# Three plain chunks per FFN instead of four, parts of 8, 7 and 7 chunks, and two of four weight mixtures formed by accumulating DMAs

## The reference

```
def swiglu(x, g, w_gu, w_down):           # D_FF = 2816 = 22 chunks of 128
    gu = rmsnorm(x, g) @ w_gu             # w_gu: 1024 x 5632
    return (silu(gu[..., :D_FF]) * gu[..., D_FF:]) @ w_down
x = x + swiglu(x, g_ffn[i], w_gu[i], w_down[i])
```

## Time and profile before

| | |
|---|---|
| median of the runs | 1291.03 us |
| the profiled execution's own time | 1293.6 us |
| its span | 1291.9 us |
| TensorE, VectorE, ScalarE, GpSimd busy | 98%, 63%, 46%, 3% |
| granted TensorE clock, mean | 0.995 of full speed |
| DMA engines' mean rate over the span | 89 GB/s |

### The profile page before, as it was taken

How to read it: one execution, slowest core, us unless ns; L and a number is a source line. 1 busy time by engine, 2 the same in 40 slices (tenths; PEclk the granted TensorE clock), 3 DMA queues, 4 the chain that set the end, 5 groups by cost and what they waited for, 6 DMA issues and landing times. The chain is left out here.

```text
span 1291.9 us, 23175 instructions
## 1 busy us (share of the span) xinstructions
PE 1260.4 (98%) x9420; PEld 1218.7 (94%) x9420; DVE 819.5 (63%) x1344; ACT 589.3 (46%) x1078; POOL 37.8 (3%) x60
## 2 busy tenths in 40 slices
PE   6999999999999999999999999999999999999997
PEld 6998999999999999999998986799999999999997
DVE  4765557964885588654654466556874786378741
ACT  6656435431552255434663467534451454155421
POOL 1000000000000000002000100000000000000011
PEclk8999999999999999999999999999999999999999
DMA  6234122232323233324443320022233223223321
GB/s 214 83 117 131 33 82 82 66 101 80 96 85 99 65 99 98 98 82 131 130 115 101 102 70 2 2 82 82 66 105 89 75 85 111 86 75 99 115 77 46
DMA packets 201969, 114.92 MB, mean 89 GB/s; under 512 B 5035, under 2 KB 198219, under 8 KB 201864
## 3 DMA queue, kind: packets, MB, share of 16 engines
q1 hardware_dynamic: 197832, 101.24, 26.6%
q0 software_dynamic: 3840, 12.15, 2.5%
q10 hardware_dynamic: 192, 0.06, 0.0%
HBM read 106.54 MB, written 6.90 MB: 88 GB/s over the span
## 5 line engine op out<-in xcount | busy, mean ns | idle before, releaser
L961 ACT ACTIVATE WH<-RAW 128x1024 fp32r<-128x1024 f32 (+2 forms) x157 | 161.2, 1027 | 271.3 <-PE ACCP L1553 271.2
L1246 DVE TENSOR_TENSOR WL<-RAW,WH 128x1024 fp32r<-128x1024 f32 (+2 forms) x157 | 186.7, 1189 | 59.5 <-ACT WH L961 58.2
L1553 PE MATMUL ACCP<-FFNH,WH 128*128 128x288 f32 x704 | 151.1, 296 | 0.0
L1553 PE MATMUL ACCP<-FFNH,WL 128*128 128x288 f32 x704 | 150.8, 296 | 0.0
L1553 PE MATMUL ACCP<-FFNL,WH 128*128 128x288 f32 x704 | 147.7, 298 | 1.3
L1442 DVE TENSOR_TENSOR X<-X,ACCP 128x288 f32<-128x288 f32 x112 | 45.8, 450 | 136.1 <-PE ACCP L1553 136.0
L1561 PE MATMUL MISC<-BH,EH 128*128 128x288 f32 x400 | 118.5, 296 | 1.4 <-DVE EL L1273 1.4
L1561 PE MATMUL MISC<-BL,EH 128*128 128x288 f32 x400 | 118.0, 295 | 0.0
L1561 PE MATMUL MISC<-BH,EL 128*128 128x288 f32 x400 | 117.6, 294 | 0.0
L1553 PE MATMUL ACCP<-XH,WH 128*128 128x288 f32 x512 | 113.6, 304 | 3.7 <-DVE XL L1326 3.7
L1553 PEld LDWEIGHTS ACCP<-FFNL,WH 128*128 128x128 f32 x704 | 111.7, 189 | 4.0 <-DVE FFNL L1482 3.6
(11 more groups left out here) (266 smaller groups left out, 2845.1 us busy)
## 6 DMA issues: line engine op xcount, KB each, us to landing
RAW<-in_w_gu SPq DMA_DIRECT2D x88, 512.0 KB, 3.6
RAW<-in_w_down SPq DMA_DIRECT2D x32, 448.0 KB, 3.9
RAW<-in_w_in SPq DMA_DIRECT2D x16, 512.0 KB, 4.1
RAW<-in_w_mem_kv SPq DMA_DIRECT2D x16, 512.0 KB, 3.9
RAW<-in_w_out SPq DMA_DIRECT2D x16, 512.0 KB, 3.9
RAW<-in_w_down SPq DMA_DIRECT2D x16, 512.0 KB, 4.2
RAW<-in_w_kv SPq DMA_DIRECT2D x8, 512.0 KB, 3.6
XR<-in_x_prompt SPq DMA_DIRECT2D x4, 512.0 KB, 6.1
```

The lines of the kernel that those rows point to most:

```text
L961: a.activation(WH[:, w % SPLIT_SLOTS, 0:nk, 0:ncol], RAW[:, p % RAW_SLOTS, 0:nk, 0:ncol], ACT.Copy).then_inc(split_ready(w, True)[0], 1)
L1246: v.tensor_tensor(WL[:, w % SPLIT_SLOTS, 0:nk, 0:ncol], RAW[:, p % RAW_SLOTS, 0:nk, 0:ncol], WH[:, w % SPLIT_SLOTS, 0:nk, 0:ncol], ALU.sub ...
L1553: ins_ = t.matmul(ACCP[0:ncol, s.g % 2, b, 0:c1_ - c0_], w[:, slot, k, 0:ncol], m[:, k, c0_:c1_], start=begin, stop=end)
```

## The change

1. LEADS goes from 4 to 3: chunk 3 of each layer becomes a pair, 19 pairs and 3 plain chunks. The preparation's table is written anew for three chunks; low parts 4, 5 and 6 move into the first pair's step (`later`).
2. PARTS goes from 7, 7, 8 chunks to 8, 7, 7. The steps `hl` inside the pairs now count from the part's first chunk.
3. For all pairs but a layer's first, mixtures 0 and 1 are no longer made by VectorE. SP loads the up panel's lower half and the gate panel's upper half into SB 0 and 1 (the addends), and POOL adds the up panel's upper half to each by an accumulating DMA from HBM. The signs of the scheme are turned so that both are sums; two preparation mixes and the product of a pair then carry a factor of -1. SP no longer loads the upper half of such an up panel into RAW.

```diff
-    PARTS = [(0, 7), (7, 14), (14, FC)]
-    LEADS = 4
+    PARTS = [(0, 8), (8, 15), (15, FC)]
+    LEADS = 3
...
-        prepare = {(0, 0): [("scale", k) for k in range(HK)], (0, 1): [("scale", HK + k) for k in range(HK)] + [("hi", 0)],
-                   (1, 0): [("mix", 1), ("mix", 2), ("hi", 1), ("hi", 2), ("hl", 0)],
-                   (1, 1): [("mix", 3), ("mix", 6), ("lo", 0), ("hi", 3), ("hi", 4)],
-                   (2, 0): [("lo", 1), ("lo", 2), ("hi", 5), ("hi", 6), ("hl", 1)],
-                   (2, 1): [("lo", 3), ("lo", 4)],
-                   (3, 0): [("lo", 5), ("lo", 6), ("hl", 2)], (3, 1): []}
+        prepare = {(0, 0): [("scale", k) for k in range(HK)], (0, 1): [("scale", HK + k) for k in range(HK)] + [("hi", 0), ("mix", 1)],
+                   (1, 0): [("mix", 2), ("hi", 1), ("hi", 2), ("mix", 3)], (1, 1): [("mix", 6), ("lo", 0), ("hi", 3), ("hi", 4)],
+                   (2, 0): [("lo", 1), ("lo", 2), ("hi", 5), ("hi", 6), ("lo", 3)], (2, 1): []}
+        later = [4, 5, 6]
...
-                if n >= 2 and j - 2 - j0 < j1 - j0 - 4:
-                    add("hl", slot=j - 2 - j0, h=layer * FC + j - 2)
+                if n >= 2 and n - 2 < j1 - j0 - 4:
+                    add("hl", slot=n - 2, h=layer * FC + j0 + n - 2)
...  (SP)
                 elif s.kind == "pair":
                     load(s.p, s.view)
-                    load(s.p + 1, s.ys)
+                    if s.alone:
+                        load(s.p + 1, s.ys)
+                    else:
+                        load(s.p + 1, lambda: s.ys()[:, HK:KC], HK)
+                        sp.wait_ge(block_lo, 5 * (s.i - 1) + 2)
+                        sp.dma_start(SB[:, 0], s.ys()[:, HK:KC]).then_inc(addend_loaded[0], 16)
+                        sp.dma_start(SB[:, 1], s.view()[:, 0:HK]).then_inc(addend_loaded[1], 16)
...  (POOL)
+                elif s.kind == "pair" and not s.alone:
+                    n = added[s.i][0] + 1
+                    for b in range(2):
+                        gp.wait_ge(addend_loaded[b], 16 * n)
+                        gp.dma_start(SB[:, b], s.ys()[:, 0:HK], accum_op=ALU.add).then_inc(sum_loaded[b], 16)
...  (ScalarE, mix_hi)
-                act.wait_ge(mixed, 4 * i + first + n)
+                summed, before = added[i]
+                if summed is None:
+                    act.wait_ge(mixed, before + first + n)
+                elif first == 0:
+                    act.wait_ge(sum_loaded[0], 16 * (summed + 1))
+                    act.wait_ge(sum_loaded[1], 16 * (summed + 1))
+                else:
+                    act.wait_ge(mixed, before + 2)
...  (VectorE)
+            def block_lo_x(layer, b):
+
+                dve.wait_ge(xc_hi, NB * layer + b + 1)
+                v.tensor_tensor(BL[:, b], term(b), BH[:, b], ALU.subtract).then_inc(xc_lo, 1)
...  (mix_2)
-                dve.wait_ge(mixed, 4 * i + 1)
-                v.tensor_tensor(SB[:, 2], SB[:, 0], raw_panel(p - 1)[:, 0:HK], ALU.subtract).then_inc(mixed, 1)
+                summed, before = added[i]
+                if summed is None:
+                    dve.wait_ge(mixed, before + 1)
+                else:
+                    dve.wait_ge(*raw_there(p - 1))
+                    dve.wait_ge(sum_loaded[0], 16 * (summed + 1))
+                    dve.wait_ge(block_lo, 5 * (i - 1) + 4)
+                v.tensor_tensor(SB[:, 2], SB[:, 0], raw_panel(p - 1)[:, 0:HK], ALU.add).then_inc(mixed, 1)
...  (hidden)
-                v.tensor_tensor(FF_[:, s.slot], TG[:], TU[:], ALU.mult).then_inc(h_ready, 1)
+                if s.kind == "pair":
+                    v.scalar_tensor_tensor(FF_[:, s.slot], TG[:], -1.0, TU[:], ALU.mult, ALU.mult).then_inc(h_ready, 1)
+                else:
+                    v.tensor_tensor(FF_[:, s.slot], TG[:], TU[:], ALU.mult).then_inc(h_ready, 1)
...  (prepare_mix 3, and 6 likewise)
-                        o = v.tensor_tensor(BT[:, 3], XN[1][:, :, right], BT[:, 1], ALU.subtract)
+                        o = v.scalar_tensor_tensor(BT[:, 3], BT[:, 1], -1.0, XN[1][:, :, right], ALU.mult, ALU.subtract)
...  (premix)
-                    mix_1(s.i, s.p)
-                    mix_3(s.i, s.p)
                     mix_2(s.i, s.p)
...  (pair, VectorE)
                         mix_lo(s.i, 2, 1)
+                        for b in s.later:
+                            block_lo_x(s.layer, b)
                         mix_lo(s.i, 3, 1)
...
-                    if s.nxt:
-                        mix_1(s.i + 1, up + 2)
-                        mix_3(s.i + 1, up + 2)
```

More of the change, by code:

```diff
@@ L57, in __init__ @@
                  q=None, i=None, slot=None, prev=None, nxt=None, alone=None, bank=None, lead=None, part=None,
-                 k=None, b=None, side=None, before=None):
+                 k=None, b=None, side=None, before=None, later=None):
         self.kind = kind
@@ L116, in __init__ @@
         self.before = before
+        self.later = later
 def encoder_kernel(nc, ins, outs):
@@ L152, in encoder_kernel @@
              "zero": 0, "win": 0, "r": 0, "h": 0, "rm": 0, "msq": 0, "pool": 0, "bank": 0,
-             "plain": 0, "split": 0, "pair": 0}
+             "plain": 0, "split": 0, "pair": 0, "added": 0}
     panel_shape, splits, raw_free = [], [], []
@@ L310, in feed_forward @@
                 left = len(pairs) - 1 - n
+                added[i] = (take("added") if i != pair0 else None), mixes[0]
+                mixes[0] += 4 if i == pair0 else 2
                 add("pair", layer=layer, i=i, p=p, sn=w, view=gate_of(j), ys=up_of(j), slot=j - j0, h=layer * FC + j,
                     prev=steps_of_pair[i - 1] if n else None, nxt=left > 0, alone=i == pair0, bank=left % 2,
-                    side=count["acc"] % 2, before=steps[-1] if i == pair0 else None, m=count["job"], g=count["acc"])
+                    side=count["acc"] % 2, before=steps[-1] if i == pair0 else None, later=later if i == pair0 else [], m=count["job"], g=count["acc"])
                 steps_of_pair[i] = steps[-1]
-                if n >= 2 and j - 2 - j0 < j1 - j0 - 4:
-                    add("hl", slot=j - 2 - j0, h=layer * FC + j - 2)
+                if n >= 2 and n - 2 < j1 - j0 - 4:
+                    add("hl", slot=n - 2, h=layer * FC + j0 + n - 2)
             add("finish", prev=steps[-1] if steps[-1].kind == "pair" else steps_of_pair[count["pair"] - 1], layer=layer,
@@ L328, in encoder_kernel @@
     steps_of_pair, rjob_of_lead = {}, {}
+    added, mixes = {}, [0]
     xsq_of = {}
@@ L670, in encoder_kernel @@
         mixed, block_hi, block_lo = sem("mixed"), sem("block_hi"), sem("block_lo")
+        addend_loaded = [sem(f"addend_loaded{b}") for b in range(2)]
+        sum_loaded = [sem(f"sum_loaded{b}") for b in range(2)]
         block_done, copied = sem("block_done"), sem("copied")
@@ L824, in _, with load @@
         def _(sp):
-            def load(p, src):
+            def load(p, src, k0=0):
                 nk, ncol = panel_shape[p]
@@ L829, in load @@
                     sp.wait_ge(*raw_released(p - RAW_SLOTS))
-                sp.dma_start(RAW[:, p % RAW_SLOTS, 0:nk, 0:ncol], src()).then_inc(raw_loaded[p % RAW_SLOTS], 16)
+                sp.dma_start(RAW[:, p % RAW_SLOTS, k0:nk, 0:ncol], src()).then_inc(raw_loaded[p % RAW_SLOTS], 16)
             for tt in range(TT):
@@ L1257, in mix_3 @@
                 dve.wait_ge(*raw_there(p - 1))
-                v.tensor_tensor(SB[:, 1], raw_panel(p - 1)[:, 0:HK], raw_panel(p)[:, 0:HK], ALU.subtract).then_inc(mixed, 1)
+                v.tensor_tensor(SB[:, 1], raw_panel(p - 1)[:, 0:HK], raw_panel(p)[:, 0:HK], ALU.add).then_inc(mixed, 1)
             def mix_2(i, p):
-                dve.wait_ge(mixed, 4 * i + 1)
-                v.tensor_tensor(SB[:, 2], SB[:, 0], raw_panel(p - 1)[:, 0:HK], ALU.subtract).then_inc(mixed, 1)
+                summed, before = added[i]
[6 more added lines that the diff above has]
+                v.tensor_tensor(SB[:, 2], SB[:, 0], raw_panel(p - 1)[:, 0:HK], ALU.add).then_inc(mixed, 1)
             def mix_4(i, p):
-                dve.wait_ge(mixed, 4 * i + 3)
-                v.tensor_tensor(SB[:, 3], raw_panel(p - 1)[:, HK:KC], SB[:, 2], ALU.subtract).then_inc(mixed, 1)
+                summed, before = added[i]
+                dve.wait_ge(mixed, before + (3 if summed is None else 1))
+                v.tensor_tensor(SB[:, 3], raw_panel(p - 1)[:, HK:KC], SB[:, 2], ALU.add).then_inc(mixed, 1)
             def mix_lo(i, first, n):
@@ L1466, in _ @@
                     if s.k == 1:
-                        o = v.tensor_tensor(BT[:, 1], XN[0][:, :, right], XN[0][:, :, left], ALU.subtract)
+                        o = v.tensor_tensor(BT[:, 1], XN[0][:, :, left], XN[0][:, :, right], ALU.subtract)
                     elif s.k == 2:
@@ L1471, in _ @@
                         dve.wait_ge(xmixed, 4 * s.layer + 1)
-                        o = v.tensor_tensor(BT[:, 3], XN[1][:, :, right], BT[:, 1], ALU.subtract)
```

(6 more changed lines are left out.)

## The result

The changed kernel takes 1375.07 us (median of 4 runs, 1373.2 to 1376.39) against 1290.99 us for the kernel before in the same comparison: a ratio of 1.0646, 95% interval [1.0633, 1.0659]. It is 84 us slower. I forecast 1296.3 us and a range up to 1316.0, so the direction was right and the size far off.

What follows compares the result with a forecast made beforehand. TensorE, busy 98% of the span, was taken as the bound. Fewer matmuls -3.2, handoff +6.8 and hidden low parts +1.7 gave +5.3 us, so 1296.3 us against 1291.03; range 1290.5 to 1316.

Steps and rivals of the forecast that it cites:

- The DMA ring: FFN pairs from pair 1 on: one buffer's round trip through SP, POOL, ScalarE and VectorE fits, so TensorE sees no wait.
- L: Ring's DMA leg, from VectorE's release through SP's addends and POOL's accumulates: taken as 8.3 us, 8.8 free.
- SP's addends: First link of the DMA leg: SP issues 0.03 us behind the release, 256 KB lands in 2.85, POOL follows 0.3 later.
- POOL's issue: Link of the DMA leg: POOL needs 0.78 us to issue one DMA.
- The transfers: Last link of the DMA leg: 256 KB lands in 3.25 us at plain rate; halved rate makes the leg 8.7.
- the far end (10.3): Upper case for the DMA leg: a slower POOL read-in of 5.5 us makes it 10.3 us.
- the ring: Rival: DMA leg over 8.8 us, so later pairs lag; 1312 us at leg 9.5, 1336 at 10.3; chance 0.24.
- The 24 matmuls: TensorE: one plain chunk per layer becomes a pair, 12 matmuls fewer at 0.1333 us each; 3.2 us less in all.
- The handoff: From plain chunks to pairs in each layer: VectorE's moved work makes TensorE wait, +3.4 us per layer, +6.8 in all.
- block 1's wait: Handoff, block 1 of pair 0: TensorE waits 1.4 us, against 0.7 before.
- The hidden low parts: Ends of down-projection parts: five low parts left in a layer's first part instead of four; +1.7 us including the slower product.
- Relieving VectorE: Later pairs: two mixtures becoming DMAs free 1.2 us of VectorE per pair; TensorE does not wait there, so no gain.

Runs made afterwards that it cites:

- the last two tuned runs: Kernel before with hidden low parts made earlier: 1289.81 us; changed kernel without DMA mixtures, preparation rearranged, hidden low parts early: 1286.67 us.
- the best order of work: Changed kernel without DMA mixtures, signs as before, three plain chunks with preparation rearranged and hidden low parts early: 1286.67 us, 0.9942 to the kernel before.

## Why the prediction was wrong

The step that failed is "The DMA ring": L was taken as 8.3 us, "nearest to the plain rows, with most of a second pass", and it is 11.4 in the median, 14.0 at most, where 8.8 were free. By its own terms:

- SP's addends: 0.03+2.85+0.3 = 3.2 us to POOL's issue; measured 3.2 in the median. Right, though nine of 36 took over 4.
- POOL's issue: taken as 0.78 from the earlier trace rows; a plain copy does take 0.75, an accumulate 1.30 (2.61 for two). Mis-sized by 0.5 us.
- The transfers: taken at the plain rate to half of it. The plain ones land in 3.4 against my 3.25, so that part was well read. An accumulate needs 2.4 times the engine time and two follow each other: together with the weights between them (0.6 us, for which the forecast had nothing), POOL's part of the leg is 8.1, where that of two plain ones is 4.9 and of two at half size 5.0. This is the mis-sized term.
- I let a slow plain read-in, 5.5 us, stand as the far end (10.3). A resource that no row shows got bounds from rows of another kind of work. The passage of the Trainium skill that I cited ("DMA: Bandwidth & Descriptors", section "Rules for kernel authors") says that an accumulate reads its destination too; I used it only to say that 8.7 would still fit, with 0.1 us to spare. The trace bears the second read out and goes beyond it: 2.4 times the engine time, not 2.

The mechanism itself stood among the rivals, with a chance of 0.24. Put the measured 11.4 into its formulas: 6 x 11.4-54.5 = 13.9 for each of four parts, 3 x 2.6+0.7 = 8.5 for each of two, 73 us; with the forecast's 5.3, 78 of 84. That this comes so near is partly luck: its waits, 73 and the handoff's 6.8, make 80 us where the trace has 60.1+7 = 67, and the forecast had no lower clock behind the longest waits, which took 14. A forecast whose margin is 0.5 us in 8.8, behind a term without a row, should have had the ring as its likeliest case, or a range that reached past its own 1336.

The other steps:
- The 24 matmuls: -3.2 forecast, 3.1 us between the last two tuned runs. Right.
- The handoff: VectorE's chain was walked forward from old rows. In the changed kernel, whose layer starts 1.0 us later:

```profile
231.66 0.68 DVE L1280 TENSOR_TENSOR SB<-RAW 128x512 f32<-128x512 f32 x1
...
236.06 2.62 DVE L1274 TENSOR_TENSOR BL<-XN,BH 128x1152 fp32r<-128x1152 f32 x2
...
242.93 0.75 DVE L1335 TENSOR_TENSOR FFNF<-GU 128x576 f32<-128x576 f32 x1
```
```profile
233.88 0.38 PE L1594 MATMUL MISC<-BH,EH 128*128 128x288 f32 x1 [1.34 <-DVE EL L1307]
```

  I had 230.7 for the first start and 242.9 for the product's end (here 231.66 and 243.68), and 1.4 for block 1's wait. Right to 0.3 us. In the run without DMAs layer 0's waits are 1.35, 0.2, 1.8 and 0.3 us where I had 1.4, 0.65, 1.4 and 0.65. That run came out at +7.5 (5.7 to 9.6 by its interval) against +5.3, although its waits are shorter than I had; its lower granted clock, for which the forecast had no term, goes the right way, but I did not isolate it.
- The hidden low parts: +1.7 forecast, +1.2 measured.
- Relieving VectorE "gives nothing": right to a microsecond. Plain copies, which relieve it as much, end at +3.2, 4 us better than with VectorE's mixtures, but only 0.9 of that is in waits for mixtures (6.1 against 7.0 us). The rest goes along with the granted clock, 0.996 to 0.997 against 0.992 to 0.995; I did not isolate it.
- Of what was to show it: the pair lasted over 11.3 us in mid-part, the sign named for the ring.

## What to carry to other kernels

Count a buffer's whole round trip against the period it must fit in, and where a link has no row in the trace, ask what a factor of two in it does before calling the margin enough. A single-buffered DMA ring turns latency into time: the same DMAs cost 76 us with one buffer, and with a second buffer, or with half as many, the kernel is at most 1 us slower than without them. They still did not pay: added to the best order of work, in two buffers, they cost 5 us. And look first at waits that a reordering removes: 4 us lay in where four small instructions stood, and another 5 in the order of the preparation, of which I changed several things together.

## What the runs showed that I had not expected

- An accumulating DMA of 256 KB in rows of 512 B goes in 528 packets, 67 ns for one of 512 B, where the plain copy of the same rows goes in 80; per byte it took 2.4 times the engine time, and POOL 1.30 us to issue against 0.75.
- Each of the eight waits of 3.0 us or more inside the changed kernel's FFNs was followed by a granted clock of 0.50 for some 3 us. Of the seven waits of 1.4 to 2.2 us one was (1.8 us, at 276), and in the run without DMAs one of two of 1.8 us; the handoff's waits of 1.3 us were not.
